# Output gate of the retention branch: computed feature-major in eight weight slots, with ungated outputs turned beforehand

## The reference

```
rq, rk, rv, rg, aq, ak, av, gr, ga = split_columns(h @ w_in, IN_WIDTHS)   # rg: 1024 columns
...
of = ret_o.astype(F32)                                  # retention outputs, 4 heads x 256
on = of * lax.rsqrt(jnp.mean(of * of, axis=-1, keepdims=True) + EPS)
r = on.reshape(B, T, RET_V) * jax.nn.silu(ret_gate)     # ret_gate = rg
br = r @ w_branch_ret
ba = att_o @ w_branch_attn
mix = jax.nn.sigmoid(gate_r) * br + jax.nn.sigmoid(gate_a) * ba
```

## Time and profile before

| | us |
|---|---|
| median of 3 runs | 1087.83 (1085.61 to 1088.73) |
| the profiled execution's own time | 1086.23 |
| its span, first to last instruction | 1084.4 |
| PE busy | 1014.0 (94%) |
| DVE busy | 541.8 (50%) |
| ACT busy | 383.5 (35%) |
| POOL busy | 197.3 (18%) |
| mean granted TensorE clock | 0.981 |

### The profile page before, as it was taken

The page is one execution under the profiler, slowest core; times in us unless marked ns, Lnnn a source line. Parts: engine busy times, 40 slices in busy tenths (PEclk is TensorE's granted clock), DMA queues, the critical chain, the costliest instruction groups (busy, mean ns, idle before and its releaser), DMA issues.

```text
span 1084.4 us, 20154 instructions
## 1 busy us (share of the span) xinstructions
PE 1014.0 (94%) x7666; PEld 882.5 (81%) x7666; DVE 541.8 (50%) x865; ACT 383.5 (35%) x842; POOL 197.3 (18%) x382
## 2 busy tenths in 40 slices
PE   5999999999997799999998888999999999999994
PEld 3777777768875699998887668999999999777773
DVE  5353233423237777765116266676667666422214
ACT  5333231441431433323223364444444443212312
POOL 2102003414133234334310100000000000011003
PEclk9999999999998899999999989999999999999998
DMA  6744425426496566564651612545554544221322
GB/s 225 263 158 161 165 102 202 175 89 232 183 297 205 167 202 200 183 203 146 228 174 59 219 59 95 208 165 174 167 202 171 174 154 145 81 84 64 112 90 85
DMA packets 40768, 175.34 MB, mean 162 GB/s; under 512 B 7242, under 2 KB 7690, under 8 KB 39168
## 3 DMA queue, kind: packets, MB, share of 16 engines
q1 hardware_dynamic: 25472, 125.78, 33.4%
q0 software_dynamic: 15232, 48.65, 14.0%
HBM read 164.40 MB, written 54.05 MB: 201 GB/s over the span
## 4 chain that ended last, share of the span: by engine, by line
PE 78%; DMA 6%; ACT 6%; DVE 5%; issue 2%; POOL 2%; SPq 0%; DVEq 0%; ACTq 0%; POOLq 0%
PE bank L1280 10%; PE bank L1282 9%; PE bank L1281 9%; PE bank L1759 8%; PE bank L1760 8%; PE bank L1761 8%; PE bank L1353 4%; PE bank L1355 4%; PE bank L1354 4%; DMA qbc<-sample_queries 3%; PE bank L1299 3%; DMA wraw<-in_weights 2%; ACT whi L782 1%; DMA kvv<-in_cache_kv_g 1%; DVE wlo L1836 1%
## 5 line engine op out<-in xcount | busy, mean ns | idle before, releaser
L1836 DVE TENSOR_TENSOR wlo<-wraw,whi 128x1024 fp32r<-128x1024 f32 x89 | 108.9, 1225 | 353.2 <-ACT whi L782 353.1
L782 ACT ACTIVATE whi<-wraw 128x1024 fp32r<-128x1024 f32 x91 | 96.4, 1059 | 391.8 <-PE bank L1282 247.6
L1759 PE MATMUL bank<-T1h,whi 128*128 128x288 f32 (+1 forms) x704 | 202.4, 288 | 3.1 <-DVE T1l L1846 1.7
L1760 PE MATMUL bank<-T1l,whi 128*128 128x288 f32 (+1 forms) x704 | 203.6, 289 | 0.0
L1761 PE MATMUL bank<-T1h,wlo 128*128 128x288 f32 (+1 forms) x704 | 203.2, 289 | 0.0
L1280 PE MATMUL bank<-whi,T1h 128*128 128x512 f32 (+1 forms) x352 | 142.3, 404 | 7.7 <-DVE etmp L1981 7.6
L1281 PE MATMUL bank<-wlo,T1h 128*128 128x512 f32 (+1 forms) x352 | 137.1, 390 | 0.0
L1282 PE MATMUL bank<-whi,T1l 128*128 128x512 f32 (+1 forms) x352 | 136.7, 388 | 0.0
L1759 PEld LDWEIGHTS bank<-T1h,whi 128*128 128x128 f32 x704 | 133.0, 189 | 3.8 <-issue 1.9
L1760 PEld LDWEIGHTS bank<-T1l,whi 128*128 128x128 f32 x704 | 132.7, 189 | 0.0
L1761 PEld LDWEIGHTS bank<-T1h,wlo 128*128 128x128 f32 x704 | 132.3, 188 | 0.0
(11 more groups left out here) (302 smaller groups left out, 1828.0 us busy)
## 6 DMA issues: line engine op xcount, KB each, us to landing
wraw<-in_weights SPq DMA_DIRECT2D x142, 512.0 KB, 3.6
out_s_kv_g<-in_cache_kv_g SPq DMA_DIRECT2D x64, 511.0 KB
qbc<-sample_queries POOLq DMA_DIRECT2D x48, 256.0 KB, 4.7
kvk<-in_cache_kv_g POOLq DMA_DIRECT2D x32, 256.0 KB, 4.3
kvv<-in_cache_kv_g POOLq DMA_DIRECT2D x16, 512.0 KB, 6.0
out_s_kv_g<-in_cache_kv_g SPq DMA_DIRECT2D x16, 508.0 KB
S<-in_state_ret POOLq DMA_DIRECT2D x16, 256.0 KB, 6.8
out_s_ret<-S POOLq DMA_DIRECT2D x16, 256.0 KB, 4.0
```

The lines of the kernel that those rows point to most:

```text
L782: nc.scalar.activation(w_halves(s)[0], wraw[:, s % 2, :], ACT.Copy).then_inc(w_hi, 1)
L1759: mm(dst, Wh, T1h[:, k, c], start=k == 0, stop=False)
L1760: mm(dst, Wh, T1l[:, k, c], start=False, stop=False)
L1836: v.tensor_tensor(lo, wraw[:, s % 2, :], hi.bitcast(F), ALU.subtract).then_inc(w_lo, 1)
```

## The change

rg is now computed by `a_tile`, one slot for 128 features, in banks 0 and 1 and 2 and 3 by turns; its sample tokens go with the others. The retention outputs are only scaled by `rs_r` in place, on ACT (`scaled_outputs`, ten activations of 256 columns for two heads), and turned ungated: `turn_outputs` behind slots 34 and 36, banks 5, 6, 7, 4, 5 for the five tiles. ACT copies the turned tiles to `oT`. The gate is then applied feature-major, slot by slot: tanh (ACT), silu (DVE), times `oT` (DVE), high part (ACT), low part (DVE). Pieces are one a slot in the gate's stage (8 in all) and 3 and 2 by turns behind it (40). The attention's last block lets PE's part of the gate on loads (w_seen) run ahead. Waits on `a_free` further down are only renumbered.

```diff
-PIECES_RG = ((0, 3, 3), (3, 3, 2))
-PIECES_GB = (1, 3, 2, 2, 2, 3, 2, 2, 2, 3, 2, 2, 2, 2, 2, 2)
+PIECES_RG = 8 * (1,)
+PIECES_GB = 8 * (3, 2)
...
-    order += [(("r", 0, i), 5 + i % 3) for i in range(TILES)]
+    order += [(("r", g, i), 4 + (i + 1) % 4) for g in range(2) for i in range(TILES)]
...
+            if bi == BLK_AV2:
+                act.wait_ge(on_sq, 20)
+                nc.scalar.activation(rt_r[:], ss_r[:], ACT.Sqrt, scale=1.0 / DV, bias=eps[:, 0:1]).then_inc(rt_ready, 1)
             dst, scales = dests[bi]
             evac_block(bi, dst, sample_dst[bi], scales)
...
+        def scaled_outputs(g):
+
+            act.wait_ge(rs_ready, 1)
+            for i in range(TILES):
+                src = vt[:, i, :] if i < 4 else vs[0:TS, :]
+                for h in (2 * g, 2 * g + 1):
+                    c = slice(DV * h, DV * h + DV)
+                    ins = nc.scalar.activation(src[:, c], src[:, c], ACT.Copy, scale=rs_r[0:rows(i), 4 * i + h:4 * i + h + 1])
+                ins.then_inc(o_ready, 1)
+
+        def turned_outputs(g):
+
+            for i in range(TILES):
+                b = filled(act, ("r", g, i))
+                n = rows(i)
+                nc.scalar.activation(oT[g][:, :, cols(i)], b[:, 0:4 * n].rearrange("p (k n) -> p k n", k=4), ACT.Copy
+                                     ).then_inc(bank_free[USES[("r", g, i)][0]], 1)
+
+        def gated_hi(k):
+
+            act.wait_ge(r_ready, k + 1)
+            nc.scalar.activation(rTh[:, k, :], gt[:, k % 4, :], ACT.Copy).then_inc(r_hi, 1)
+
+        for q in range(4):
+            act.wait_ge(s1_out[q], 16 * RH)
+        act.wait_ge(k_out, 16 * (NG + 2))
+        scaled_outputs(0)
+        for s in range(8):
+            if s in (1, 3):
+                turned_outputs(s // 2)
+            w_split(S_RG + s + 2)
+            if s == 2:
+                scaled_outputs(1)
+            act.wait_ge(w_used, S_RG + s + 1)
+            if s >= 4:
+                act.wait_ge(r_lo, s - 3)
+            for half in range(2):
+                ins = nc.scalar.activation(gt[:, s % 4, HALF * half:HALF * half + HALF], P[2 * (s % 2) + half][:, 0:HALF],
+                                           ACT.Tanh, scale=0.5)
+            ins.then_inc(e_ready, 1)
+            if s:
+                gated_hi(s - 1)
+        gated_hi(7)
...
+        for s in range(8):
+            pe.wait_ge(w_lo, S_RG + s + 1)
+            if s < 2:
+                pe.wait_ge(b_free[2 * s], BLK_AV2 + 1)
+                pe.wait_ge(b_free[2 * s + 1], BLK_AV2 + 1)
+            else:
+                pe.wait_ge(a_free[s % 2], s // 2)
+            a_tile(S_RG + s, T1h, T1l, KT, 2 * (s % 2)).then_inc(w_used, 1)
+            if s in (0, 2):
+                pe.wait_ge(b_free[4], BLK_AV2 + 1)
+                turn_outputs(s // 2)
...
             if s == 1:
-                for i in (0, 1, 2):
-                    emptied(pe, ("r", 1, i))
+                pe.wait_ge(r_lo, 8)
...
+        def gated_output(k):
+
+            if k in (0, 4):
+                for i in range(TILES):
+                    emptied(dve, ("r", k // 4, i))
+            dve.wait_ge(a_free[k % 2], k // 2 + 1)
+            v.tensor_tensor(gt[:, k % 4, :], gt[:, k % 4, :], oT[k // 4][:, k % 4, :], ALU.mult).then_inc(r_ready, 1)
+
+        def gated_lo(k):
+
+            dve.wait_ge(r_hi, k + 1)
+            v.tensor_tensor(rTl[:, k, :], gt[:, k % 4, :], rTh[:, k, :].bitcast(F), ALU.subtract).then_inc(r_lo, 1)
+
+        for s in range(8):
+            w_split(S_RG + s + 2)
+            dve.wait_ge(e_ready, s + 1)
+            for half in range(2):
+                c = slice(HALF * half, HALF * half + HALF)
+                ins = v.scalar_tensor_tensor(gt[:, s % 4, c], gt[:, s % 4, c], 1.0, P[2 * (s % 2) + half][:, 0:HALF],
+                                             ALU.add, ALU.mult)
+            ins.then_inc(a_free[s % 2], 1)
+            if s:
+                gated_output(s - 1)
+            if s >= 2:
+                gated_lo(s - 2)
+            for _ in range(PIECES_RG[s]):
+                sample_piece()
+        gated_output(7)
+        gated_lo(6)
+        gated_lo(7)
```

More of the change, by code:

```diff
@@ L67 @@
 BLOCKS = ([(S_RET + 4 * n, 4, 2, 512) for n in range(4)] + [(S_ATT + 4 * n, 4, 2, 512) for n in range(4)]
-          + [(S_ATT + 16, 2, 4, 256)] + [(S_RG + 4 * n, 4, 2, 512) for n in range(2)]
+          + [(S_ATT + 16, 2, 4, 256)]
           + [(S_OUT + 4 * n, 4, 2, 512) for n in range(2)] + [(S_DN + 11 * n, 11, 2, 512) for n in range(2)])
-BLK_RQ, BLK_RK, BLK_RV, BLK_AQ, BLK_AQK, BLK_AK, BLK_AV, BLK_AV2, BLK_RG, BLK_OUT, BLK_DN = 0, 1, 2, 4, 5, 6, 7, 8, 9, 11, 13
+BLK_RQ, BLK_RK, BLK_RV, BLK_AQ, BLK_AQK, BLK_AK, BLK_AV, BLK_AV2, BLK_OUT, BLK_DN = 0, 1, 2, 4, 5, 6, 7, 8, 9, 11
 ROPE_BLOCKS = (BLK_RQ, BLK_RK, BLK_AQ, BLK_AQK, BLK_AK)
@@ L104, in value_piece @@
     return 2 * q + e, g
-PIECES_RG = ((0, 3, 3), (3, 3, 2))
-PIECES_GB = (1, 3, 2, 2, 2, 3, 2, 2, 2, 3, 2, 2, 2, 2, 2, 2)
-assert sum(map(sum, PIECES_RG)) + sum(PIECES_GB) == 48
+PIECES_RG = 8 * (1,)
+PIECES_GB = 8 * (3, 2)
+assert sum(PIECES_RG) + sum(PIECES_GB) == 48
 def psum_uses():
@@ L151 @@
 USES = psum_uses()
-SPLIT_KEYS = [k for k in USES if k[0] in ("x", "r", "h2")]
+SPLIT_KEYS = [k for k in USES if k[0] in ("x", "h2")]
 SPLIT_NO = {k: n for n, k in enumerate(SPLIT_KEYS)}
@@ L325, in build_layer @@
     pT = sb("pT", at, [128, 2, 512]); at += 1024
-    qbc = [sb(f"qbc{n}", at + 512 * n, [128, 2, 256]) for n in range(3)]
+    qbc = [sb(f"qbc{n}", SCR + 2176 + 512 * n, [128, 2, 256]) for n in range(3)]
+    assert 4 * NTOK <= 2176 and 2176 + 1536 <= 3840
     at = SCR + 3840
@@ L943, in sample_outputs_evac @@
                                  accum_out=ss_r[0:TS, 16 + h:17 + h]).then_inc(on_sq, 1)
-        for bi in range(BLK_RG):
+        for bi in range(BLK_OUT):
             first, n = BLOCKS[bi][:2]
@@ L970, in _ @@
                 sample_outputs_evac(bi - 4)
[L971 to L998, removed]
@@ L1032, in _ @@
                 exponentials(n)
-                if s == 0:
-                    for i in range(TILES):
-                        split_evac(("r", 1, i), rTh, None, 4, i)
             elif n:
@@ L1465, in between, with turn_outputs @@
                     retention_part(bi - 4, s)
-            b_block(bi, *(T1_by_class if bi == BLK_AV else T1), between=between, ready=x_ready if bi == 0 else None)
-        def turn_gated(g):
+            b_block(bi, *(T1_by_class if bi == BLK_AV else T1), between=between, ready=x_ready if bi == 0 else None,
+                    ahead=S_OUT - S_RG if bi == BLK_AV2 else 0)
+        def turn_outputs(g):
             for i in range(TILES):
-                pe.wait_ge(r_ready, 5 * g + (i + 2 if i < 4 else 1))
+                pe.wait_ge(o_ready, 5 * g + i + 1)
                 r = rows(i)
@@ L1971, in _ @@
                 step(v.reciprocal(rs_r[:], rt_r[:]))
[L1973 to L1992, removed]
+                v.tensor_scalar(rs_r[:], rs_r[:], 0.5, None, ALU.mult).then_inc(rs_ready, 1)
         pieces = itertools.count()
@@ L2296, in weight_stream @@
     parts.append(b_slots(att[:, 2048:], 4))
-    parts += [b_slots(rg[:, 512 * n:512 * n + 512], 2) for n in range(2)]
+    parts.append(a_slots(rg))
     parts.append(np.stack([a_slots(gr), a_slots(w_branch_ret)], 1).reshape(-1, 128, SLOT))
```

41 lines of the change are left out of this document (13 added, 28 removed).

## The result

After: median 1081.66 us (1078.54 to 1083.76, 11 runs), before in the same session 1087.83 us (1083.33 to 1090.89, 11 runs). The ratio is 0.9943, 95% interval 0.9931 to 0.9956. The profiled execution took 1079.33 us, its span is 1077.5, against 1084.4.

What follows compares the result with a forecast made beforehand. The stage was bound by what DVE has ahead of PE's needs: 81.5 us less 60.6 of PE work gives 20.9, minus 10.9 waits and 4.4 clock, a 5.6 us gain from 1087.83 to 1082.2 us, range 1079.5 to 1084.5.

Steps and rivals of the forecast that it cites:

- What bounds the stage: Last attention projection matmul to first reading gated outputs, 81.5 us: bound by what DVE has ahead of PE's needs.
- second idle time: PE's 6.1 us without work at the turned halves in the kernel before, put down to late piece loads.
- PE's work, 60.6 us: Stage after the change without waits: eight slots 49.1 us, turns 4.4, slot 42 with first scores 7.1.
- rival 4: Short matmuls cost by instruction, not column: gate's product 13 us more, 7.4 us lost, 1095 us; chance 0.02.
- Wait A: Behind slot 34, PE's fifth turned tile waits for bank 5 until ACT copies the first: 2.8 us.
- Wait B: Behind slot 36, PE's turns wait for scaled outputs, then bank 5: 6.8 us over the turns' 2.2.
- Wait C: At slot 43, PE waits for the low part of the eighth tile: 8.4 us against 7.1, so 1.3.
- Clock: Slow PE clock after idle times: 1.7 us lost behind Wait A, 2.7 behind Wait B, 4.4 off the gain.
- Six pieces at zero: Pieces moved behind slot 42, 8.7 us of DVE over eight slot pairs, costed at nothing; bounds 0 and 8.7.
- Rival 3: Three piece buffers bind in slots 42 to 57, each pair 2.5 us longer: 1101 us; chance 0.08.
- PE's wait behind slot 58: PE's wait for all pieces, claimed to stay, since the last piece remains first behind the last gate.

Runs made afterwards that it cites:

- e4: Kernel before with only the pieces recounted as in the changed kernel (none in first gate block, 8 in second, 5 to two slots behind): 1079.32 us, ratio 0.9916.
- e6: Kernel before with no pieces in the gate's stage and six to two slots behind it: 1082.09 us, ratio 0.9947.
- e5: Changed kernel with both halves' turned tiles copied ahead of tanh and the second half scaled behind slot 34's tanh: 1070.30 us, ratio 0.9842.
- e11: The kernel of e5 run again, beside e12 on the same chip: 1070.87 us, ratio 0.9845.
- e2: Changed kernel with the second half's outputs scaled behind slot 35's tanh, not behind the split of slot 38: 1080.28 us, ratio 0.9932.
- e7: Changed kernel with no pieces in the gate's stage and six to two slots behind it: 1087.22 us, ratio 0.9990.
- e9: Changed kernel with pieces shared out as before the change, 14 in the gate's stage and 34 behind: 1080.84 us, ratio 0.9933.
- e10: Kernel before with the gate stage's eight pieces moved from in front of the first turned halves, 40 behind the stage: 1081.41 us, ratio 0.9944.
- e3: Changed kernel with both halves' turned tiles copied ahead of tanh and the second half scaled behind slot 35's tanh: 1071.11 us, ratio 0.9833.
- e12: The kernel of e3 run again, beside e11 on the same chip: 1072.78 us, ratio 0.9863.
- e8: Changed kernel with a dummy one-column tanh ahead of the first scaled copies, so the table load comes earlier: 1078.96 us, ratio 0.9911.

## Why the prediction was right

The forecast was 1082.2 us, a gain of 5.6; measured were 1081.66 us, and 6.9 us in the span.

- **What bounds the stage** (DVE's list, with late pieces ahead of what PE needs): confirmed. e4 and e6 take pieces out of it without touching the form, and the old form's stage falls from 81.8 to 75.2 and 67.8 us. The pieces were not all of it: 2.13 us of the second idle time stay without any (e6).
- **PE's work, 60.6 us**: confirmed by e5 and e11, which have almost nothing else in the stage: 60.2. The first slot's 48 matmuls took 6.02 us (298.46 to 304.48), 0.125 each, so the gate's product went by columns, and rival 4 is out. By "TensorE: Matmul & The Clock Gate" of the Trainium skill (Back-to-back issue gap), as the prediction read it, the stage would have been 13 us longer; the traces of this case don't agree: matmuls of 272 columns start 0.125 us apart and those of 512 columns 0.23 (e4, 320 to 322 us), nearly in the ratio of their columns.
- **Wait A, 2.8 us**: 3.17. The scaled copy was 0.41 us, as estimated; the norm scale was ready at 301.88 instead of 301.4. The prediction's chain is ACT's timeline above, entry by entry. The drain that "ScalarE: Activation LUTs" of the Trainium skill (What ACT_TABLE_LOAD costs) adds to the load was on neither side of it: the split ahead ends at 306.93, the load runs from 306.95 to 308.23, the tanh begins at 308.24.
- **Wait B, 6.8 us over the turns' own 2.2, so 9.0 from the end of slot 36**: 9.1 (323.6 to 332.7). e2 shows that its two parts hide each other, e5 that both are order alone.
- **Wait C, 1.3 us**: 0.80. Mis-sized by 0.5: I added the durations of DVE's operations, but successive ones start before the one ahead has ended in the rows. This error and A's 0.4 the other way nearly cancel.
- **Clock, 1.7 and 2.7 us**: 1.7 and 2.8. For A that was luck. The forecast took half of 3.4 us because it could not choose between nothing and all; what came was neither, but half clock for half as long (matmuls 0.225 us apart from 311.1 to 314.3, then 0.125 again). B fell as it did behind the long idle times before.
- **Six pieces at zero**: nearly right for slots 42 to 57, the cover less wide than I wrote. I counted 4.2 us of idle DVE time a pair against 1.1 us more of pieces. The ring's loads took nearly all of it (DVE's idle time before the low parts: 25.5 us, then 1.3). Rival 3, a ring that makes every pair longer, did not come: landings stayed at 4.6 us at the median, and in e6, with one more piece a pair, only the first pair stood. What six a pair do cost is that one late score maximum with its half clock, some 5 us (e6, e7). And PE's wait behind slot 58 did not stay as it was, as I had written: its part for `qbd` went from 2.29 to 3.06 us.

What the prediction did not see: its gain has two sufficient causes. The change of form alone (e9) gives 6.4 us of stage, the pieces alone (e4) give 6.6, both together 6.6. They don't add, because each ends at its own next limit: in the new form waits A and B, in the old one the second idle time. So that the forecast came out does not show that the form gave the gain; the pieces alone would have given it. The form is worth more only once ACT's order is put right. Then it gives 62.4 us with eight pieces in the stage, which is less than the 67.8 of the old form with none.

## What to carry to other kernels

When a change brings both a new form and new places for side work, run each alone before crediting either: here each gave the whole gain, and two reorderings of ACT's list, with no new operation, then gave 11 us more. Put into an in-order engine's list first what another engine waits for, and put preparations at the step where all that stands ahead of them is already ready, not at the latest one. Side work moved out of a tight place moves its wait too: look at what stands behind it where it lands (e6, e10).

## What was not expected of the hardware

Half clock came after short idle times, and not for the same time. Behind wait B of e3, idle 1.65 us between turns, and behind the same wait of e12, idle 1.66 us, the stretches read (columns as above; first e3, then e12):

```profile
324.20:331.00 6.80, 6.80 (x32) 6.74 (x33) 3.98 (x7) 2.66 (x7) 1.09 (x2) 0.51 0.37 127
```

```profile
324.30:325.40 1.10, 1.08 (x10) 1.06 (x11) 0.66 (x1) 1.10 (x3) 0.00 (x0) 1.00 0.85 231
325.40:328.80 3.40, 3.40 (x18) 3.40 (x17) 2.45 (x5) 1.57 (x5) 0.00 (x0) 0.51 0.47 160
```

That is 3.3 us lost in one execution and 1.7 in the other, of one kernel and one idle time. The 1.17 us of wait A in e5 lost nothing, and neither did 1.63 us at the same place in e8 nor 2.13 us at the turned halves in e6. Before, 2.0 us without a matmul had lost nothing and 2.3 us had lost 3.4. So the price of a wait of 1.6 to 3.2 us lay between nothing and 3.4 us on top of the wait, and a single trace shows one draw of it. Why 1.65 us cost what 1.63, 2.0 and 2.13 us did not is open.
